# One-hot tiles of eight tokens per VectorE compare in the expert-gate scatter of a PEER block, and the gates as a second pass

## The chip, the cores and the metric

The kernel runs on one core of one Trainium2 chip, in one launch. The metric is the device time of that launch in microseconds (us), the median of repeated runs; lower is better. All data are float32. The engines are TensorE (PE; its weight loads are listed as PEld), VectorE (DVE), ScalarE (ACT), GpSimd (POOL) and SyncE (SP), which issues most DMAs.

## The reference, cut to what matters

The whole model is one block of gated linear attention with a PEER layer and two blocks of attention with a convolutional feed-forward, over 512 tokens of width 1024. The change lies in the PEER layer. For each of 512 tokens, 8 retrieval heads pick 16 experts each out of 128 x 128 = 16,384 by product keys, so that a token has 128 selected experts with a softmax gate each:

```python
expert = (jnp.take_along_axis(i1, top_c // PEER_TOPK, axis=-1) * PEER_N_KEYS
          + jnp.take_along_axis(i2, top_c % PEER_TOPK, axis=-1))
gate = jax.nn.softmax(top_s, axis=-1)
...
act = jax.nn.gelu(jnp.einsum("pd,ped->pe", xb, jnp.take(u, eb, axis=0)), approximate=False)
return jnp.einsum("pe,ped->pd", (gb * act).astype(v.dtype), jnp.take(v, eb, axis=0))
```

An expert's number is e1 * 128 + e2. The kernel treats 384 of the tokens (TD) densely: it computes the activations of all 16,384 experts and multiplies them by a dense matrix of gates, zero for experts not selected. The other 128 tokens are gathered row by row.

## The kernel before, in words

Each engine's program is written out by hand, stage after stage; the engines meet at semaphores (`wait_ge(name, key)`, `inc(name, key)`), and each engine executes its instructions in the written order. `after(stage, ...)` makes an engine wait for the end of a stage on the others. The stages around the change are *retrieve* (queries, key scores, the top-16 searches, expert numbers), *spread* (the stage that is changed) and *experts* (the dense products over 64 blocks of 256 experts).

**The work of the spread stage.** It makes, for each dense token t, the 128 x 128 matrix of its gates. `e1T`, `e2T` and `gT` are 128 x 384 tiles: partition s holds, in column t, the two halves of the number and the gate of the token's s-th selected expert. `iota` holds 0 to 127 along each partition's row. Two one-hot tiles of 128 x 128 are made: `oa` is 1 where iota equals e1T's column t, multiplied by the gate gT; `ob` is 1 where iota equals e2T's column. One float32 matmul of the two, over the 128 selections, gives the token's gates; four tokens share a PSUM bank `B[q % 8]` (q counts groups of four, 96 in all). ScalarE copies each bank into `stage` (written token-last), and SyncE stores a full stage of 32 tokens (BT) to DRAM (`gd`), whence the experts stage loads it (`gt`).

**Who makes what, before.** There are 24 buffers of 128 x 128 for `oa` and 24 for `ob` (NOH). VectorE makes every `oa` in one instruction (compare, then multiply by the gate; two scalar columns). The `ob` of a token goes by `t % 16`: 5 of 16 to ScalarE (two instructions, |iota - e2| and relu(1 - that)), 3 of 16 to VectorE, 8 of 16 to GpSimd. Each instruction signals, TensorE waits for both tiles of a token, and a buffer is free again when the matmul of 24 tokens before is done. ScalarE's order is that of `spread_order()`: the `ob` tiles of four tokens, two groups of four ahead, then the copy of one bank. GpSimd first issues four indirect DMAs (`own_row_pool`, L2185), which wait for the expert numbers of the other 128 tokens.

The neighbouring lines which the text uses: L1908, L1929, L1944 and L1948 are the retrieve stage's broadcast operations of 128 x 1024 elements (`ge`, `eq`), of which VectorE and GpSimd each take some; L196 splits weights; L499 is a VectorE multiply with accumulation, and L2329 is GpSimd's multiply of activations by gates, both in the experts stage. L234 is the common matmul line.

Of the kernel before, what the change touches and what calls it, by code (L numbers as in the profile page):

```python
# [7 lines left out]
ALU = mybir.AluOpType  # L8
ACT = mybir.ActivationFunctionType
# [11 lines left out]
T = TX + TC  # L21
# [8 lines left out]
BT = 32  # L30
# [107 lines left out]
def spread(ap, n):  # L138
    return ap.unsqueeze(2).to_broadcast([ap.shape[0], ap.shape[1], n])
# [1510 lines left out]
TD = 384  # L1650
# [28 lines left out]
def peer_plan(k):  # L1679
    m = k.m  # L1680
    k.U2 = m.pair("Up", [128, KC, TX])
    k.own = Net()
    k.own.x = m.sb("ownx", [128, D])
    k.own.at, k.own.atf = m.sb("ownat", [128, NSLOT], U32), m.sb("ownatf", [128, NSLOT])
    k.own.gate, k.own.dot, k.own.w = (m.sb("own", [128, NSLOT]) for _ in range(3))
    own_u = m.top
    k.own.u = [m.sb("ownu", [128, D]) for _ in range(NUB)]
    top = m.top
    k.n2 = NormMod(k, "n2", k.X, k.sc2, k.MOD[0][:, 24:32, :], k.U2, (XR,), sums_at=own_u, sums=4, rows=3)
    m.top = top  # L1690
    k.peer_top = m.top
    k.iota, k.marks = m.sb("iota", [128, 128]), m.sb("marks", [128, 32])
    k.e1T, k.e2T, k.gT = (m.sb("eT", [128, TD]) for _ in range(3))
    top2 = m.top
    k.R = Retrieval(k)
    m.top = top2
    k.oa = [m.sb("oa", [128, 128]) for _ in range(24)]
    k.ob = [m.sb("ob", [128, 128]) for _ in range(24)]
    k.stage = [m.sb("stage", [128, 128, BT]) for _ in range(2)]
    m.top = top  # L1700
    k.gt = [m.sb("gt", [128, TD // BT, 4, BT]) for _ in range(2)]
    k.acts = [m.pair("act", [128, 2, TD]) for _ in range(2)]
    k.ge = [m.sb("ge", [128, TD]) for _ in range(2)]
    k.own.acc = k.X[:, 0:4, TX:T]
    side = m.top
    k.side = [m.sb("side", [128, TW]) for _ in range(2)]
    k.cb2 = m.sb("cb", [128, 2 * D])
    k.dots3 = Dots(k, "experts", k.cb2, k.X[:, 4:8, TX:T])
    k.own.v = [m.sb("ownv", [128, D]) for _ in range(NVB)]
    end, m.top = m.top, side  # L1710
    k.ot = [m.sb("ot", [128, D]) for _ in range(3)]
    m.top = end
# [341 lines left out]

def expert_engine(t):

    if t % 16 in (1, 5, 7, 11, 13):
        return "act"  # L2060
    return "dve" if t % 16 in (3, 8, 14) else "pool"


NOH = 24


def spread_order():

    out = [("hot", t) for t in range(8)]
    for q in range(TD // 4):  # L2070
        if q + 2 < TD // 4:
            out += [("hot", t) for t in range(4 * q + 8, 4 * q + 12)]
        out.append(("group", q))
    return out


def spread_pe(k):
    pe = k.pe
    for q in range(TD // 4):
        b = k.B[q % 8]  # L2080
        if q >= 8:
            pe.wait_ge("staged", q - 8)
        for i in range(4):
            t = 4 * q + i
            pe.wait_ge("hot_a", t)
            if expert_engine(t) == "act":
                pe.wait_ge("hot_act", t)
            elif expert_engine(t) == "dve":
                pe.wait_ge("hot_dve", t)
            else:  # L2090
                pe.wait_ge("hot_pool", t)
            ins = pe.e.matmul(b[:, i * 128:(i + 1) * 128], k.ob[t % NOH][:], k.oa[t % NOH][:], start=True, stop=True)  # L2092
            ins.then_inc(*pe.inc("mm", ("hot", t)))
    pe.mark("spread")


def spread_act(k):
    a = k.act
    a.after("retrieve", "pe", "dve", "pool")
    for what, t in spread_order():  # L2100
        if what == "hot":
            if expert_engine(t) == "act":
                ob = k.ob[t % NOH]
                if t >= NOH:
                    a.wait_ge("mm", ("hot", t - NOH))
                a.e.activation(ob[:], k.iota[:], ACT.Abs, bias=k.e2T[:, t:t + 1], scale=-1.0).then_inc(*a.inc("hot_act", (t, 0)))
                a.wait_ge("hot_act", (t, 0))
                a.e.activation(ob[:], ob[:], ACT.Relu, bias=k.one[:, 0:1], scale=-1.0).then_inc(*a.inc("hot_act", t))
        else:
            n, i0 = 4 * t // BT, 4 * t % BT  # L2110
            a.wait_ge("mm", ("hot", 4 * t + 3))
            if n >= 2:
                a.wait_ge(f"stored{n % 2}", n - 2)
            a.e.activation(k.stage[n % 2][:, :, i0:i0 + 4], k.B[t % 8].rearrange("p (t i) -> p i t", t=4), ACT.Copy).then_inc(
                *a.inc("staged", t))
    a.mark("spread")


def spread_dve(k):
    v = k.dve  # L2120
    v.after("retrieve", "pe", "act", "pool")
    v.wait_ge("chosen", ("T", 2))
    for t in range(TD):
        if t >= NOH:
            v.wait_ge("mm", ("hot", t - NOH))
        v.e.tensor_scalar(k.oa[t % NOH][:], k.iota[:], k.e1T[:, t:t + 1], k.gT[:, t:t + 1], ALU.is_equal, ALU.mult).then_inc(
            *v.inc("hot_a", t))
        if expert_engine(t) == "dve":
            v.e.tensor_scalar(k.ob[t % NOH][:], k.iota[:], k.e2T[:, t:t + 1], None, ALU.is_equal).then_inc(*v.inc("hot_dve", t))
    v.mark("spread")  # L2130


def spread_pool(k):
    g = k.pool
    g.after("retrieve", "pe", "act", "dve")
    for s in range(NUB):
        own_row_pool(k, "u", s)
    for t in range(TD):
        if expert_engine(t) == "pool":
            if t >= NOH:  # L2140
                g.wait_ge("mm", ("hot", t - NOH))
            g.e.tensor_scalar(k.ob[t % NOH][:], k.iota[:], k.e2T[:, t:t + 1], None, ALU.is_equal).then_inc(*g.inc("hot_pool", t))
    g.mark("spread")


def spread_sp(k):
# [31 lines left out]
def own_row_pool(k, which, s):  # L2178

    g, S = k.pool, k.own  # L2180
    g.wait_ge("own", "at")
    if which == "u":
        if s >= NUB:
            g.wait_ge("own_dot", s - NUB)
        g.e.indirect_dma_start(S.u[s % NUB][:], None, k.dram["un"], bass.IndirectOffsetOnAxis(S.at[:, s:s + 1], 0)).then_inc(  # L2185
            *g.inc(f"own_u{s % NUB}", s, by=16))
    else:
        if s >= NVB:
            g.wait_ge("own_sum", s - NVB)
        g.e.indirect_dma_start(S.v[s % NVB][:], None, k.dram["vn"], bass.IndirectOffsetOnAxis(S.at[:, s:s + 1], 0)).then_inc(  # L2190
            *g.inc(f"own_v{s % NVB}", s, by=16))
# [1813 lines left out]
def tensor_program(k):  # L4005
# [9 lines left out]
    n2_pe(k)  # L4015
    retrieve_pe(k)
    spread_pe(k)
    experts_pe(k)
    join_pe(k)
# [18 lines left out]
def scalar_program(k):  # L4038
# [8 lines left out]
    n2_act(k)  # L4047
    retrieve_act(k)
    spread_act(k)
    experts_act(k)  # L4050
    join_act(k)
# [19 lines left out]
def vector_program(k):  # L4071
# [8 lines left out]
    n2_dve(k)  # L4080
    retrieve_dve(k)
    spread_dve(k)
    experts_dve(k)
    join_dve(k)
# [19 lines left out]
def gpsimd_program(k):  # L4104
# [9 lines left out]
    n2_pool(k)  # L4114
    retrieve_pool(k)
    spread_pool(k)
    experts_pool(k)
    join_pool(k)
# [34 lines left out]
def make_plan(k):  # L4153
# [32 lines left out]
    assert m.top <= heads  # L4186
    m.top = base
    peer_plan(k)
    m.top = base
    k.r64, k.r96 = m.sb("r64", [128, 128]), m.sb("r96", [128, 128])  # L4190
# [247 lines left out]
```

## Time and profile before

| | |
|---|---|
| median of 3 runs | 5478.99 us (5473.9 to 5482.6) |
| the profiled execution | 5479.94 us |
| its span | 5478.6 us |
| granted TensorE clock over the span | 0.951 |
| spread stage: first one-hot to the next stage's first matmul | 1324.43 to 1465.00 us |

Times in the trace count from the span's start. Busy time of an engine is the sum over its instructions. PEclk, the granted clock, is a share of TensorE's full speed of 2.4 GHz; it has two levels, 0.5 and 1.0, and a value between them is a mixture over the stretch. Some instructions of an engine overlap by a fraction of a microsecond, so that the distance from start to start is shorter than the duration.

### The profile page before, as it was taken

The numbers are of one execution on the slowest core, as the hardware profiler recorded it, in microseconds if no ns is written. First come the engines' busy times: TensorE is split into PE (matmuls) and PEld (weight loads), VectorE is DVE, ScalarE is ACT, GpSimd is POOL, SyncE is SP. The second block draws the span as 40 slices with busy tenths as digits, with TensorE's granted clock in tenths as the row PEclk, the third lists the DMA queues.
The fourth block names the chain that finished last, engine by engine and source line by source line (L and its number), as shares of the span: only waits on it lengthen the run. The fifth ranks groups of instructions, "written<-read, shape, count | busy, mean of one in ns | idle before, by whom it ended". The sixth has DMA issues, their size and how long they took to land.

```text
span 5478.6 us, 67230 instructions
## 1 busy us (share of the span) xinstructions
PE 4942.2 (90%) x27217; PEld 4153.0 (76%) x27217; DVE 3122.6 (57%) x5388; ACT 1909.0 (35%) x2822; POOL 1176.5 (21%) x1003
## 2 busy tenths in 40 slices
PE   7998899965899999999789988979999799899999
PEld 7887777754788888888667776768888667777787
DVE  5444455579767777775444555555444544444545
ACT  3445522223733333333341423313222343333333
POOL 1111100025644545442120002200000120021000
PEclk8999999987999999999899999999999899999999
DMA  3111023412588888884103012121111101112221
GB/s 151 52 53 63 24 100 125 152 40 76 228 276 303 305 301 301 303 284 167 55 24 124 28 70 75 61 113 62 58 63 62 44 24 67 39 48 93 78 98 71
DMA packets 157444, 638.39 MB, mean 117 GB/s; under 512 B 12384, under 2 KB 62577, under 8 KB 106321
## 3 DMA queue, kind: packets, MB, share of 16 engines
q1 hardware_dynamic: 112528, 467.97, 24.1%
q0 software_dynamic: 42528, 162.98, 8.5%
q8 instruction: 217, 3.56, 0.3%
q10 hardware_dynamic: 2080, 3.15, 0.2%
q14 instruction: 91, 0.74, 0.0%
HBM read 597.35 MB, written 36.70 MB: 116 GB/s over the span
## 4 chain that ended last, share of the span: by engine, by line
PE 75%; DVE 10%; ACT 7%; issue 3%; DMA 3%; POOL 2%; DVEq 0%; SPq 0%; ACTq 0%; POOLq 0%
PE banks L234 63%; PE banks L2793 2%; PE banks L2892 1%; PE banks L2798 1%; DVE cols L2824 1%; ACT P L2842 1%; PE banks L2919 1%; PE banks L962 1%; DVE raw L499 1%; DVE prod L499 1%; PE banks L355 1%; PE banks L2092 1%; PE banks L308 1%; DMA X<-ctxT_in 1%; PE banks L894 1%
## 5 line engine op out<-in xcount | busy, mean ns | idle before, releaser
L234 PE MATMUL banks<-UH,spl1H 128*128 128x512 f32 (+1 forms) x1600 | 591.6, 370 | 46.6 <-issue 16.7
L196 DVE TENSOR_TENSOR spl0L<-raw,spl0H 128x2048 fp32r<-128x2048 f32 (+3 forms) x171 | 370.9, 2169 | 424.2 <-ACT spl0H L181 377.9
L234 PE MATMUL banks<-UL,spl1H 128*128 128x512 f32 (+1 forms) x1600 | 583.3, 365 | 0.0
L234 PE MATMUL banks<-UH,spl1L 128*128 128x512 f32 (+1 forms) x1600 | 582.4, 364 | 0.0
L196 DVE TENSOR_TENSOR spl1L<-raw,spl1H 128x2048 fp32r<-128x2048 f32 (+1 forms) x170 | 379.2, 2231 | 344.4 <-ACT spl1H L181 341.4
L234 PE MATMUL banks<-UH,spl0H 128*128 128x512 f32 (+2 forms) x1184 | 434.0, 367 | 41.1 <-issue 12.7
L181 ACT ACTIVATE spl1H<-raw 128x2048 fp32r<-128x2048 f32 (+1 forms) x170 | 313.5, 1844 | 440.5 <-PE banks L234 280.8
L181 ACT ACTIVATE spl0H<-raw 128x2048 fp32r<-128x2048 f32 (+3 forms) x171 | 306.2, 1790 | 422.7 <-PE banks L234 202.0
L234 PE MATMUL banks<-UL,spl0H 128*128 128x512 f32 (+2 forms) x1184 | 427.9, 361 | 0.0
L234 PE MATMUL banks<-UH,spl0L 128*128 128x512 f32 (+2 forms) x1184 | 427.2, 361 | 0.0
L234 PE MATMUL banks<-UpH,spl0H 128*128 128x384 f32 (+1 forms) x1072 | 370.7, 346 | 44.2 <-issue 23.0
L234 PEld LDWEIGHTS banks<-UH,spl1H 128*128 128x128 f32 x1600 | 306.0, 191 | 107.1 <-issue 47.3
L234 PE MATMUL banks<-UpL,spl0H 128*128 128x384 f32 (+1 forms) x1072 | 367.8, 343 | 0.0
L234 PE MATMUL banks<-UpH,spl0L 128*128 128x384 f32 (+1 forms) x1072 | 367.6, 343 | 0.0
L234 PEld LDWEIGHTS banks<-UH,spl1L 128*128 128x128 f32 x1600 | 305.9, 191 | 51.7
L234 PEld LDWEIGHTS banks<-UL,spl1H 128*128 128x128 f32 x1600 | 306.4, 191 | 50.4 <-issue 0.8
L234 PE MATMUL banks<-spl1H,actH 128*128 128x512 f32 x756 | 299.4, 396 | 15.5 <-issue 15.5
L2824 DVE TENSOR_REDUCE cols<-banks 128x1 f32<-128x768 f32 (+3 forms) x240 | 190.7, 795 | 189.5 <-PE banks L2798 106.0
L234 PE MATMUL banks<-spl1L,actH 128*128 128x512 f32 x756 | 298.3, 395 | 0.0
L234 PE MATMUL banks<-spl1H,actL 128*128 128x512 f32 x756 | 298.2, 394 | 0.0
L234 PEld LDWEIGHTS banks<-UH,spl0H 128*128 128x128 f32 (+1 forms) x1184 | 225.7, 191 | 87.0 <-issue 38.9
L3962 POOL TENSOR_TENSOR cv<-cv 128x768 f32<-128x768 f32 (+1 forms) x44 | 69.0, 1569 | 922.5 <-DVE cv L3933 922.5
(477 smaller groups left out, 11560.9 us busy)
## 6 DMA issues: line engine op xcount, KB each, us to landing
raw<-uT_in SPq DMA_DIRECT2D x64, 1024.0 KB
raw<-ev_in SPq DMA_DIRECT2D x64, 1024.0 KB
raw<-up_in SPq DMA_DIRECT2D x44, 1024.0 KB
raw<-ada_in SPq DMA_DIRECT2D x40, 1024.0 KB
gd<-stage SPq DMA_DIRECT2D x12, 2048.0 KB, 6.6
gt<-gd SPq DMA_DIRECT2D x32, 768.0 KB, 7.3
side<-ada_in SPq DMA_DIRECT2D x24, 1024.0 KB, 6.6
raw<-gate_in SPq DMA_DIRECT2D x24, 1024.0 KB
```

The costliest lines, as they stand in the source:

```text
L181: a.e.activation(k.spl[i % SPL].h[:, 0:w], k.raw[j % RAW][:, 0:w], ACT.Copy).then_inc(*a.inc("w_hi", j))
L196: v.e.tensor_tensor(s.l[:, 0:w], k.raw[j % RAW][:, 0:w], s.h[:, 0:w].bitcast(F32), ALU.subtract).then_inc(*v.inc("w_lo", j))
L234: ins = pe.e.matmul(out, x, y, start=start and i == 0 and j == 0, stop=stop and i == n - 1 and j == 2)
L308: ins = pe.e.matmul(s.sums[:, o:o + 1], s.sq[i % len(s.sq)][:, c * 128:(c + 1) * 128], k.ones[:, 0:1], start=(i == 0 and c == 0), stop=(j ...
L355: ins = pe.e.matmul(b[:, c * 128:(c + 1) * 128], k.ones[:], d[:, c, :], start=True, stop=True)
L499: v.e.scalar_tensor_tensor(x if r else S.out, x, 1.0, w, ALU.mult, ALU.mult, accum_out=MOD[:, 2 * t + c, r:r + 1]).then_inc(*v.inc("dot", ...
L894: ins = pe.e.matmul(state_at(H, d, gi, c), w.kdT[r:r + 64, c // 2, :], v[r:r + 64, c // 2, :], start=True, stop=True)
L962: ins = pe.e.matmul(o[:, c * 64:(c + 1) * 64], w.S[:, c, x * 128:(x + 1) * 128], w.qd[:, c * 64:(c + 1) * 64], start=False, stop=(c == ord ...
L2092: ins = pe.e.matmul(b[:, i * 128:(i + 1) * 128], k.ob[t % NOH][:], k.oa[t % NOH][:], start=True, stop=True)
L2793: ins = pe.e.matmul(k.W[1 + j][:, at:at + n], Q[lo:hi, q * 128:(q + 1) * 128], K[lo:hi, k0:k0 + n], start=True, stop=True)
L2824: v.e.reduce_max(mx, src, AX_X).then_inc(*v.inc("largest", (tag, i, j)))
L3962: g.e.tensor_tensor(va[:, 0:w], va[:, 0:w], ga[:, 0:w], ALU.mult).then_inc(*g.inc("ffn_prod", (l, j)))
```

## The change

The 24 + 24 small buffers become 3 + 3 buffers of eight tokens each (NHOT, HOT; the same memory). VectorE makes `oa` of eight tokens in one `tensor_tensor` compare of 128 x 1024 elements, both inputs read from SBUF with broadcasts: iota repeated over the eight tokens, e1T's column repeated over 128 elements. The gate is no longer part of it: for 29 of the 48 groups VectorE multiplies `oa` by gT in a second `tensor_tensor`, for the other 19 ScalarE scales the eight pieces in place, one instruction each. `ob` comes from GpSimd for 22 groups (eight `tensor_scalar` instructions as before, one signal behind the eighth) and from VectorE for 26 (one compare of 128 x 1024). ScalarE makes no one-hots any more. TensorE has the same 384 matmuls, waits once for a group of eight, and signals once in four.

```diff
-    k.oa = [m.sb("oa", [128, 128]) for _ in range(24)]
-    k.ob = [m.sb("ob", [128, 128]) for _ in range(24)]
+    k.oa, k.ob = ([m.sb(n, [128, HOT, 128]) for _ in range(NHOT)] for n in ("oa", "ob"))
...
+HOT, NHOT = 8, 3
...
+def second_on_pool(g):
+
+    return g % 2 == 0 and g % 24 != 22
...
+def gates_on_act(g):
+
+    return g % 5 in (1, 3)
...
+def tokens_of(x, g):
+
+    return spread(x[:, g * HOT:(g + 1) * HOT], 128)
...
 def spread_pe(k):
...
+        if gates_on_act(g):
+            pe.wait_ge("hot_act", g)
+        else:
+            pe.wait_ge("hot_gate", g)
+        if second_on_pool(g):
+            pe.wait_ge("hot_pool", g)
+        else:
+            pe.wait_ge("hot_dve", g)
         for i in range(4):
...
+            t = 4 * (q % 2) + i
+            ins = pe.e.matmul(b[:, i * 128:(i + 1) * 128], k.ob[g % NHOT][:, t, :], k.oa[g % NHOT][:, t, :], start=True, stop=True)
+        ins.then_inc(*pe.inc("mm", ("hot", q)))
...
+def gates_act(k, g):
+
+    a = k.act
+    if g < TD // HOT and gates_on_act(g):
+        a.wait_ge("hot_a", g)
+        for t in range(HOT):
+            o = k.oa[g % NHOT][:, t, :]
+            ins = a.e.activation(o, o, ACT.Copy, scale=k.gT[:, g * HOT + t:g * HOT + t + 1])
+        ins.then_inc(*a.inc("hot_act", g))
...
+    for q in range(TD // 4):
+        if q % 2 == 0:
+            gates_act(k, q // 2 + 2)
...
-    for t in range(TD):
-        if t >= NOH:
-            v.wait_ge("mm", ("hot", t - NOH))
-        v.e.tensor_scalar(k.oa[t % NOH][:], k.iota[:], k.e1T[:, t:t + 1], k.gT[:, t:t + 1], ALU.is_equal, ALU.mult).then_inc(
-            *v.inc("hot_a", t))
-        if expert_engine(t) == "dve":
-            v.e.tensor_scalar(k.ob[t % NOH][:], k.iota[:], k.e2T[:, t:t + 1], None, ALU.is_equal).then_inc(*v.inc("hot_dve", t))
+    io = k.iota[:].unsqueeze(1).to_broadcast([128, HOT, 128])
+    for g in range(TD // HOT):
+        oa, ob = k.oa[g % NHOT], k.ob[g % NHOT]
+        if g >= NHOT:
+            v.wait_ge("mm", ("hot", 2 * (g - NHOT) + 1))
+        v.e.tensor_tensor(oa[:], io, tokens_of(k.e1T, g), ALU.is_equal).then_inc(*v.inc("hot_a", g))
+        if not second_on_pool(g):
+            v.e.tensor_tensor(ob[:], io, tokens_of(k.e2T, g), ALU.is_equal).then_inc(*v.inc("hot_dve", g))
+        if not gates_on_act(g):
+            v.wait_ge("hot_a", g)
+            v.e.tensor_tensor(oa[:], oa[:], tokens_of(k.gT, g), ALU.mult).then_inc(*v.inc("hot_gate", g))
...
+    for g in range(TD // HOT):
+        if second_on_pool(g):
+            if g >= NHOT:
+                p.wait_ge("mm", ("hot", 2 * (g - NHOT) + 1))
+            for t in range(HOT):
+                ins = p.e.tensor_scalar(k.ob[g % NHOT][:, t, :], k.iota[:], k.e2T[:, g * HOT + t:g * HOT + t + 1], None, ALU.is_equal)
+            ins.then_inc(*p.inc("hot_pool", g))
```

VectorE's instructions from the start of the spread stage on, before (line, operation, output and inputs, elements, count in a row; `eT` is any of e1T, e2T and gT):

```order
L2126 TENSOR_SCALAR oa<-iota,eT 128x128 x4
L2129 TENSOR_SCALAR ob<-iota,eT 128x128
L2126 TENSOR_SCALAR oa<-iota,eT 128x128 x5
L2129 TENSOR_SCALAR ob<-iota,eT 128x128
L2126 TENSOR_SCALAR oa<-iota,eT 128x128 x6
L2129 TENSOR_SCALAR ob<-iota,eT 128x128
```

VectorE's instructions at the same place in the changed kernel:

```order
L2133 TENSOR_TENSOR oa<-iota,eT 128x1024
L2138 TENSOR_TENSOR oa<-oa,eT 128x1024
L2133 TENSOR_TENSOR oa<-iota,eT 128x1024
L2135 TENSOR_TENSOR ob<-iota,eT 128x1024
L2133 TENSOR_TENSOR oa<-iota,eT 128x1024
L2138 TENSOR_TENSOR oa<-oa,eT 128x1024
```

The first six rows held 15 + 3 instructions on 128 x 128 elements, one tensor input each; now six instructions with two tensor inputs each cover the groups 0 to 2, which are 24 tokens. The group 1 has its gates from ScalarE, the groups 0 and 2 their `ob` from GpSimd.

ScalarE's instructions from the start of the stage on, before:

```order
L2106 ACTIVATE ob<-iota,eT 128x128
L2108 ACTIVATE ob<-ob,one 128x128
L2106 ACTIVATE ob<-iota,eT 128x128
L2108 ACTIVATE ob<-ob,one 128x128
L2106 ACTIVATE ob<-iota,eT 128x128
L2108 ACTIVATE ob<-ob,one 128x128
L2106 ACTIVATE ob<-iota,eT 128x128
L2108 ACTIVATE ob<-ob,one 128x128
L2114 ACTIVATE stage<-banks 128x128x4
```

And in the changed kernel:

```order
L2102 ACTIVATE oa<-oa,eT 128x128 x8
L2119 ACTIVATE stage<-banks 128x128x4 x2
L2102 ACTIVATE oa<-oa,eT 128x128 x8
L2119 ACTIVATE stage<-banks 128x128x4 x6
L2102 ACTIVATE oa<-oa,eT 128x128 x8
```

The pairs that made `ob` are gone; eight scalings in a row stand ahead of every fourth or sixth copy of a bank.

## Rows read from the trace of the kernel before

**Rows 1.** Windows: busy us and count by engine, then granted clock, DMA share.

```profile
core 0: us, PE busy (x) PEld busy (x) DVE busy (x) ACT busy (x) POOL busy (x), PEclk, DMA share, GB/s
1340.00:1360.00 20.00, 16.99 (x116) 14.24 (x116) 19.46 (x74) 19.41 (x51) 20.00 (x33) 1.00 0.44 182
```

**Rows 2.** Groups of instructions, 1324 to 1466 us: busy us, mean ns, idle before.

```profile
L2142 POOL TENSOR_SCALAR ob<-iota,eT 128x128 f32<-128x128 f32 x192 | 121.5, 646 | 4.9 <-PE banks L2092 4.6
L2126 DVE TENSOR_SCALAR oa<-iota,eT 128x128 f32<-128x128 f32 x384 | 115.9, 358 | 7.3 <-PE banks L2092 6.2
L2114 ACT ACTIVATE stage<-banks 128x512 f32<-128x512 f32 x96 | 55.4, 579 | 6.6 <-PE banks L2092 6.5
L2129 DVE TENSOR_SCALAR ob<-iota,eT 128x128 f32<-128x128 f32 x72 | 21.5, 299 | 0.0
```

**Rows 3.** Timeline, one period of 16 tokens on TensorE: start, length, count.

```profile
1374.53 5.03 PE L2092 MATMUL banks<-oa,ob 128*128 128x128 f32 x32 [0.52 <-ACT ob L2108]
1380.09 5.03 PE L2092 MATMUL banks<-oa,ob 128*128 128x128 f32 x32 [0.53 <-ACT ob L2108]
1457.83 0.97 PEld L2092 LDWEIGHTS banks<-oa,ob 128*128 128x128 f32 x8 [0.69 <-issue]
```

**Rows 4.** Timeline at the start and the end of the spread stage.

```profile
1324.43 1.11 DVE L2126 TENSOR_SCALAR oa<-iota,eT 128x128 f32<-128x128 f32 x4
1324.91 0.40 ACT L2108 ACTIVATE ob<-ob,one 128x128 f32<-128x128 f32 x1
1325.21 0.39 ACT L2106 ACTIVATE ob<-iota,eT 128x128 f32<-128x128 f32 x1
1330.27 20.14 POOL L2142 TENSOR_SCALAR ob<-iota,eT 128x128 f32<-128x128 f32 x32
1463.17 1.78 ACT L2114 ACTIVATE stage<-banks 128x512 f32<-128x512 f32 x3
1465.00 0.44 PE L234 MATMUL banks<-UpH,spl1H 128*128 128x384 f32 x1 [0.69 <-ACT stage L2114]
```

**Rows 5.** Timeline, VectorE and GpSimd operations of 128 x 1024 in retrieve.

```profile
1307.10 1.21 DVE L1929 TENSOR_TENSOR eq<-small,iota 128x1024 f32<-128x1024 f32 x1
1308.22 1.21 DVE L1935 TENSOR_REDUCE ex<-eq 128x64 f32<-128x1024 f32 x1
1308.39 2.34 POOL L1948 TENSOR_TENSOR eq<-eq,small 128x1024 f32<-128x1024 f32 x1 [6.19 <-DVE eq L1929]
1309.35 2.46 DVE L1908 TENSOR_TENSOR ge<-small,marks 128x1024 f32<-128x1024 f32 x1
1317.28 1.16 DVE L1929 TENSOR_TENSOR eq<-small,iota 128x1024 f32<-128x1024 f32 x1
1318.48 1.23 DVE L1948 TENSOR_TENSOR eq<-eq,small 128x1024 f32<-128x1024 f32 x1
```

**Rows 6.** Timeline, GpSimd behind a VectorE operation; then both in the experts stage.

```profile
1277.49 2.28 DVE L196 TENSOR_TENSOR spl1L<-raw,spl1H 128x2048 fp32r<-128x2048 f32 x1
1277.64 4.33 POOL L1944 TENSOR_TENSOR ge<-ge,small 128x1024 f32<-128x1024 f32 x1 [1.16 <-DVE ge L1908]
...
2452.87 1.22 DVE L499 SCALAR_TENSOR_TENSOR X<-side,cb 128x1024 f32<-128x1024 f32 x1
2452.87 2.09 POOL L2329 TENSOR_TENSOR ge<-ge,gt 128x384 f32<-128x384 f32 x1 [1.02 <-ACT ge L2294]
2454.12 1.91 DVE L499 SCALAR_TENSOR_TENSOR side<-side,cb 128x1024 f32<-128x1024 f32 x1
```

**Rows 7.** Instructions by line: durations ns min/median/max, first and last start.

```profile
L2142 POOL TENSOR_SCALAR ob<-iota,eT x192: 592/636/827, 1330.3 to 1456.0; 128x128 f32<-128x128 f32 x192
L2129 DVE TENSOR_SCALAR ob<-iota,eT x72: 273/301/395, 1325.5 to 1455.8; 128x128 f32<-128x128 f32 x72
L1944 POOL TENSOR_TENSOR ge<-ge,small x7: 2337/4357/4422, 1158.3 to 1299.9; 128x1024 f32<-128x1024 f32 x7
```

**Rows 8.** Windows of the retrieve stage: busy us by engine, granted clock.

```profile
1150.00:1200.00 50.00, 37.18 (x162) 30.37 (x160) 43.86 (x250) 10.58 (x20) 18.53 (x22) 0.83 0.12 43
```

## What the change does to the time, forecast from the trace

> **What bounds the kernel now.** I looked first at the stage that is touched. It runs from VectorE's first one-hot at 1324.43 to the next stage's first matmul at 1465.00 [rows 4]: 140.6 us, 2.6% of the span. Outside it the change alters nothing but line numbers, so the whole effect lies in when that last matmul starts. Then the windows: in 20 us of steady state ScalarE is busy 19.41, VectorE 19.46, GpSimd 20.00 and TensorE 16.99 [rows 1]. Three engines are full at once, and that is the first thing to see: no engine can be relieved alone. The timeline shows who ends the waits: the 16-token pattern repeats after 1380.09 - 1374.53 = 5.56 us, and each new period on TensorE begins at an `ob` of ScalarE [rows 3]; 24 periods are 133.4 us. The rest is the start, where GpSimd compares only from 1330.27 on, behind its four indirect DMAs [rows 4]. TensorE itself could be quicker: the eight weight loads of four tokens take 0.97 us when nothing holds them up [rows 3], so 384 tokens need some 93 us.
>
> **ScalarE.** Its 240 one-hot instructions go. It gets 19 x 8 = 152 scalings; like instructions follow each other after 1325.21 - 1324.91 = 0.30 us [rows 4], which is 46 us, and the bank copies stay at 55.4 us [rows 2]. Together 101 us in a stage of 140: it stops being the bound. The work goes to VectorE.
>
> **VectorE by itself.** Its 384 + 72 instructions, 137.4 us of overlapping durations [rows 2], become 48 + 26 compares and 29 multiplies of 128 x 1024, 103 in all. The price is shown by the same shapes with the same broadcasts: from a compare to an independent instruction 1308.22 - 1307.10 = 1.12 us, and 1318.48 - 1317.28 = 1.20 us to a multiply that waits for that compare [rows 5]. So 74 x 1.12 + 29 x 1.20 = 117.7 us if nothing disturbs it. That is nearly what its part of the stage is now; the eightfold instruction saves little, since the gate becomes a second pass.
>
> **VectorE against GpSimd: the term that decides.** The old VectorE instructions read one tensor, the new ones two. Wherever a VectorE instruction with two inputs in SBUF meets a GpSimd `tensor_tensor`, the trace shows one of them standing still. The `ge` compare began at 1309.35 under a GpSimd multiply that ended at 1308.39 + 2.34 = 1310.73, and took 2.46 us, ending 1.08 after it; the reduction under the same multiply took its plain 1.21 [rows 5]. The other way round, GpSimd's multiply began at 1277.64 under a VectorE subtraction that ended at 1279.77, and ended 2.20 us later, where the fastest of its kind takes 2.337 in all [rows 6, 7]: only 0.14 us was hidden. In the experts stage they alternate: GpSimd ends 0.87 after VectorE, and VectorE's next 1.07 after GpSimd [rows 6]. Such pairs add up instead of overlapping.
>
> That is what the Trainium skill says in "SBUF — State Buffer", under "Who interferes with whom": a VectorE instruction with two SBUF inputs contends with a GpSimd instruction that reads SBUF, and the pair of ports is held for the whole instruction. The rows just read agree, for `tensor_tensor` on GpSimd. By the rule the sum would be the upper of the two below.
>
> No row shows a GpSimd `tensor_scalar`, of which 22 x 8 = 176 remain, against two inputs on VectorE. Its cost is bounded from both sides. Upper: it shuts VectorE out as its `tensor_tensor` does, for 0.592 [rows 7] less the hidden 0.14, 0.45 us. Lower: the one-input compares of VectorE that share the stage with exactly these GpSimd instructions, which fill all of the stretch [rows 1], range from 273 to 395 ns [rows 7], so they never waited more than 0.12 us. Nothing at all is a rival of its own (below).
>
> Now the sum. Up to 1330.3 GpSimd issues DMAs and VectorE gets 5 instructions done (5.9 us at 1.12 to 1.20); 98 remain. As long as both have work they take turns, since each waiting one is served when the other ends: one GpSimd instruction per VectorE instruction, 1.08 + h us. That handles 98 of GpSimd's 176; the other 78 run while VectorE waits for a buffer, at 0.60 us each (between the least, 0.592, and the median, 0.636 [rows 7]), 46.8 us. VectorE does have to wait: the ring has three groups, group g + 3 needs the matmuls of g, and those need GpSimd's eight pieces. GpSimd seldom waits, since its next group is g + 2, in the buffer of g - 1.
>
> - h = 0.45: 98 x 1.53 + 46.8 = 196.7, the last one-hot at 1527.0.
> - h = 0.12: 98 x 1.20 + 46.8 = 164.4, at 1494.7.
>
> Behind it come eight matmuls, 2 x 0.97 = 1.9 us, and the last copy of a bank, 1.78 / 3 = 0.6 us [rows 3, 4], with signals 3 us, against 1465.00 now: +65 and +33 us. The row on the very instruction speaks for short, those on two inputs for long; with nothing nearer I take the middle, h = 0.29: 98 x 1.37 + 46.8 = 181.1, next stage at 1514.4, +49 us. Startup costs nothing beyond this: group 0 is complete when GpSimd has made eight pieces, and TensorE has slack. Fewer signals and waits on TensorE are costed at nothing, being covered by the same wait for one-hots; if the cover were gone, the floor of 93 us is still far below.
>
> The profiled execution is 5479.94, 1 us above the median of the runs. 5479.9 + 49 = 5529 against that execution, and 5528 against the median of 5478.99.
>
> **The rivals.**
>
> 1. *No contention with `tensor_scalar`* (ends on the other side). For it: GpSimd's 192 compares now run with a median of 636 against a least of 592 ns beside a full VectorE [rows 7], although some of VectorE's are slowed. Against it: GpSimd's operand comes through the same memory as its `tensor_tensor`'s. VectorE's 117.7 us then are the bound. At the start it is ahead by three groups at about 1331.3 and waits for group 0: 1330.3 + 8 x 0.60 + 1.9 = 1337.0, 6 us idle. The next stage starts at 1324.4 + 117.7 + 6 + 3 = 1451, 14 us earlier; GpSimd needs 4.8 of each 4.9 us for 16 tokens, so part of it may go in ring waits. 5466 to 5480. It decides if GpSimd shuts VectorE out for less than some 0.02 us per instruction. Chance 0.14: faster 0.08, same 0.06.
> 2. *GpSimd is stopped twice in an instruction*, once for the scalar column and once for the row, and gets through one in two VectorE instructions. Then 49 are done beside the 98, and 127 alone: 98 x 1.20 + 127 x 0.60 = 193.8 (+62 us) to 98 x 1.53 + 76.2 = 226.1 (+95 us). All that speaks for it is the long duration of each (0.592 us for 128 elements); no row shows two stops. 5541 to 5574. Chance 0.12.
> 3. *TensorE becomes the bound at the lower clock level.* Its bursts of 1.9 us would fill 3.9 of 7.5 us per 16 tokens, half; in retrieve, at 37.18 us busy of 50, the granted clock was 0.83, a mixture of both levels [rows 8]. At 1.2 GHz throughout, 16 tokens take 4 x 2 x 0.97 = 7.8 us, 24 times 186 us: about +55 us. It hides under the main forecast and adds some 5 us. Chance 0.06.
> 4. *Little changes*: VectorE's turns cost about h = 0.12, and two GpSimd instructions fit between two of VectorE's, so that the 78 alone shrink to few: 98 x 1.2 + 10 = 128 to 140, -2 to +12 us. 5478 to 5491. Chance 0.06: same 0.04, slower 0.02.
>
> **How the numbers follow.** The main case, one GpSimd instruction per VectorE instruction and an added wait between the bounds, has 0.62: 5512 to 5545. It and rivals 2 and 3 are slower throughout, as is a third of rival 4. Two kernels of this length can be told apart from about 0.2%, 11 us. That gives faster 0.08, same 0.10, slower 0.82. The range goes from 5475, which takes in rival 4 and the upper half of rival 1, to 5565, two thirds of rival 2: about 0.1 is left out below and 0.05 above.
>
> **What the profile would show.** Right: VectorE's 128 x 1024 compares in the stage with a median well above 1.22 us (1.3 to 1.7), and GpSimd's compares above 0.64, up to 1.5 us; the sum of VectorE's and GpSimd's busy time inflated by waits; TensorE busy at about half in the stage, its waits ended by GpSimd's `ob`; ScalarE idle a third of it. The stage 174 to 206 us long, all other stages as they were. Wrong: VectorE's compares at 1.2 and GpSimd's at 0.6 side by side, which is rival 1; GpSimd's at over 1.7 us, rival 2. The forecast also fails if the two do not take turns, one of them holding the other off for long runs; then the sum stays but the split between the two kinds of wait changes.

## The result, and the profile after

The changed kernel takes 5552.23 us (median of 4 runs, 5546.34 to 5552.93) against 5479.42 us: a ratio of 1.0136, 95% interval 1.0120 to 1.0152. The forecast was 5528 with a range to 5565: right in direction, and 24 us short in size. 5552 lies outside the 5512 to 5545 of the main case and inside the 5541 to 5574 of rival 2.

The stage, from the windows of the profile after (columns as in [rows 1]), and the waits of the stage (who waited for whom: us in total, times, longest us):

```profile
core 0: us, PE busy (x) PEld busy (x) DVE busy (x) ACT busy (x) POOL busy (x), PEclk, DMA share, GB/s
1361.00:1381.00 20.00, 12.78 (x91) 12.62 (x90) 12.99 (x12) 10.36 (x27) 18.88 (x18) 0.74 0.25 106
```

```profile
PE banks L2090 <- POOL ob L2152: 92.2, 13, 13.5
DVE oa L2133 <- PE banks L2090: 84.6, 15, 9.5
ACT oa L2102 <- DVE oa L2133: 36.4, 19, 12.4
POOL ob L2152 <- PE banks L2090: 17.0, 10, 6.5
```

Where three engines were full [rows 1], GpSimd alone is nearly so now (18.88 of 20 us). TensorE waits 92.2 us for its one-hots, VectorE 84.6 us for TensorE to free a buffer; VectorE and ScalarE are idle a third and a half of the time. The stage ran from 1324.51 to 1536.47 us, 211.96 in place of 140.57 [rows 4]: 71.4 of the 72.8 us by which the span grew. The rest of the kernel took 0.1 us more ahead of the stage and 1.3 us more behind it.

The groups of the stage after, against [rows 2]:

```profile
L2152 POOL TENSOR_SCALAR ob<-iota,eT 128x128 f32<-128x128 f32 x176 | 176.5, 1024 | 17.0 <-PE banks L2090 17.0
L2133 DVE TENSOR_TENSOR oa<-iota,eT 128x1024 f32<-128x1024 f32 x48 | 59.0, 1235 | 84.8 <-PE banks L2090 84.6
L2138 DVE TENSOR_TENSOR oa<-oa,eT 128x1024 f32<-128x1024 f32 x29 | 36.0, 1243 | 0.5
L2135 DVE TENSOR_TENSOR ob<-iota,eT 128x1024 f32<-128x1024 f32 x26 | 33.8, 1300 | 0.0
```

Fewer GpSimd compares than before (176 for 192) are busy for longer (176.5 for 121.5 us), while VectorE's are hardly above their 1.21 us. Read one by one, VectorE and GpSimd in the same 5 us:

```profile
1346.45 1.21 DVE L2133 TENSOR_TENSOR oa<-iota,eT 128x1024 f32<-128x1024 f32 x1
1347.58 1.30 DVE L2135 TENSOR_TENSOR ob<-iota,eT 128x1024 f32<-128x1024 f32 x1
1348.81 1.21 DVE L2138 TENSOR_TENSOR oa<-oa,eT 128x1024 f32<-128x1024 f32 x1
1349.95 1.30 DVE L2133 TENSOR_TENSOR oa<-iota,eT 128x1024 f32<-128x1024 f32 x1
```

```profile
1345.67 2.38 POOL L2152 TENSOR_SCALAR ob<-iota,eT 128x128 f32<-128x128 f32 x1
1348.03 2.38 POOL L2152 TENSOR_SCALAR ob<-iota,eT 128x128 f32<-128x128 f32 x1
```

A GpSimd compare ends every 2.36 us, one for two VectorE instructions, and every second VectorE instruction is 0.09 us longer. The compare that began at 1345.67 outlasted the instruction that VectorE was in (to 1346.52) and the whole next one (to 1347.66), and ended 0.39 us after that. Over the 176 records: 52 lasted over 1.3 us, together 105.4 us; the other 124 took 0.60 each, 74.7 us. With 17.0 us of waits, less 3.7 us by which neighbours overlap, that is the 193.4 us from the first to the last (1332.5 to 1525.9). It is rival 2, counted beforehand as 49 beside VectorE and 127 alone.

### The profile page after: what moved, and what is told of

It is laid out like the page before. It is cut to its first block, busy times and chain, and to the rows that moved or that the text cites. A ratio compares the mean times of both kernels' runs of the same rounds, so it can differ in the third digit from the quotient of the medians.

```text
span 5551.4 us, 66438 instructions
## 1 busy us (share of the span) xinstructions
PE 4947.1 (89%) x27217; PEld 4173.1 (75%) x27217; DVE 3121.5 (56%) x5035; ACT 1877.3 (34%) x2734; POOL 1233.0 (22%) x987
## 4 chain that ended last, share of the span: by engine, by line
PE 78%; DVE 8%; ACT 6%; POOL 4%; issue 3%; DMA 2%; DVEq 0%; ACTq 0%; POOLq 0%; SPq 0%
PE banks L234 64%; POOL ob L2152 2%; PE banks L2804 2%; PE banks L2903 1%; PE banks L2809 1%; PE banks L2090 1%; ACT P L2853 1%; DVE cols L2835 1%; PE banks L2930 1%; PE banks L962 1%; PE banks L308 1%; PE banks L355 1%; DMA X<-ctxT_in 1%; PE banks L894 1%; PE banks L953 1%
```

## The experiments

Theory A: a VectorE instruction with two inputs in SBUF keeps GpSimd out while it runs. Theory B: the hand-over of eight tokens in a ring of three groups costs the time. The stage's length below goes from VectorE's first one-hot to the next stage's first matmul, as in [rows 4]. The kernel before was run again beside the experiments: medians of 5473.84, 5473.88 and 5473.88 us, and 5474.09 in the single run that belongs to the constant for the scalar column. That is 5 to 6 us below the 5479.42 beside the changed kernel, so differences in total between experiments are taken from each one's own kernel before (the changed kernel: 72.8 us above). Where no ratio is given, the experiment is a single run and is judged by its stage.

**One input, by scalar columns.**

```diff
-        v.e.tensor_tensor(oa[:], io, tokens_of(k.e1T, g), ALU.is_equal).then_inc(*v.inc("hot_a", g))
+        v.e.tensor_scalar(oa[:], io, k.e1T[:, g * HOT:g * HOT + 1], k.one[:, 0:1], ALU.is_equal, ALU.mult).then_inc(*v.inc("hot_a", g))
...
```

> The changed kernel, but VectorE's instructions of the stage read one tensor in place of two: compares and gate multiplies of 128 x 1024 take scalar columns (one of the group's first token, one of ones). Left out: all eight tokens of a group get the first one's column. Theory A (a second SBUF input on VectorE keeps GpSimd out of its reads): GpSimd's compares at 0.60 us with none over 0.8, its indirect DMA issues back at 0.95 us, VectorE's instructions about 1.2 us, the stage 126 to 132 us in place of 211, total 5465 to 5475. Theory B (the coarse hand-over of eight tokens in a ring of three groups costs the time, whoever reads what): the stage stays above 190 us, total above 5530.

5503.75 us, the stage 164.9 us: neither. The edit changed more than it was meant to:

```profile
L2133 DVE TENSOR_SCALAR oa<-iota,eT,one x48: 799/816/1222, 1327.1 to 1485.9; 128x1024 f32<-128x1024 f32 x48
L2152 POOL TENSOR_SCALAR ob<-iota,eT x176: 590/597/1717, 1333.2 to 1483.1; 128x128 f32<-128x128 f32 x176
```

VectorE read 1024 elements in 0.80 us instead of 1.21, and 63 GpSimd compares lasted over 0.7 and up to 1.72 us. So one input is not enough to leave GpSimd alone. The Trainium skill, "VectorE: DVE Perf Modes", section "Mode 2×_2P — use both read ports for one tensor", says that an instruction with one tensor input can read the two halves of that tensor through both read ports at once, on float32 too; the 0.80 us agree. As a test of the second input the run decides nothing.

**One input, at the same 1.21 us.**

```diff
-        v.e.tensor_tensor(oa[:], io, tokens_of(k.e1T, g), ALU.is_equal).then_inc(*v.inc("hot_a", g))
+        if g < NHOT:
+            v.e.tensor_tensor(oa[:], io, tokens_of(k.e1T, g), ALU.is_equal).then_inc(*v.inc("hot_a", g))
+        else:
+            v.e.tensor_reduce(oa[:, :, 0], io, AX_X, ALU.add).then_inc(*v.inc("hot_a", g))
...
```

> The changed kernel, but from group 3 on each VectorE instruction of the stage is a reduction over the same 128 x 1024 elements of iota, which reads one tensor, one element per cycle, and writes eight elements per partition. Left out: the compares and multiplies of these groups. Theory A: with the same 1.2 us instructions but one input, GpSimd's compares stay at 0.60 us, none above 0.8 after group 2; stage 120 to 131 us, some 10 us below the kernel before. In the run with one input and scalar columns VectorE's instructions fell to 0.81 us, two elements per cycle, and GpSimd was still held up; if it is VectorE's being busy with long instructions as such that holds GpSimd up, here too a third of its compares last over 1.3 us and the stage stays above 165 us.

5467.72 us, the stage 131.8 us, 1 us beyond the forecast's end:

```profile
L2136 DVE TENSOR_REDUCE oa<-iota x45: 1209/1210/1222, 1342.0 to 1450.9; 128x8 f32<-128x1024 f32 x45
L2163 POOL TENSOR_SCALAR ob<-iota,eT x176: 590/607/652, 1333.4 to 1446.0; 128x128 f32<-128x128 f32 x176
```

The same 1.21 us on VectorE, the same ring and groups of eight, and no GpSimd compare above 0.652. So VectorE's being busy does not hold GpSimd up, and theory B falls. The reduction differs in what it writes, too, so by itself this does not yet name the second input.

**The second input from PSUM.** The whole computation is kept.

```diff
+RING = (0, 1, 3, 4, 5, 6, 7)
...
-        b, g = k.B[q % 8], q // 2
-        if q >= 8:
-            pe.wait_ge("staged", q - 8)
+        b, g = k.B[RING[q % 7]], q // 2
+        if q >= 7:
+            pe.wait_ge("staged", q - 7)
...
-    io = k.iota[:].unsqueeze(1).to_broadcast([128, HOT, 128])
+    v.e.tensor_copy(k.B[2][:, TD:TX], k.iota[:]).then_inc(*v.inc("iota_bank", 0))
+    v.wait_ge("iota_bank", 0)
+    io = k.B[2][:, TD:TX].unsqueeze(1).to_broadcast([128, HOT, 128])
...
-            v.e.tensor_tensor(oa[:], oa[:], tokens_of(k.gT, g), ALU.mult).then_inc(*v.inc("hot_gate", g))
+            v.e.tensor_tensor(oa[:], oa[:], tokens_of(k.B[2], g), ALU.mult).then_inc(*v.inc("hot_gate", g))
```

> The changed kernel, computing all of it, but VectorE's second input comes from PSUM: iota is copied to the last quarter of bank 2 and the gates are read where the transposes left them in the same bank; the four-token results go round the other seven banks. Theory A (only a second input from SBUF keeps GpSimd out): GpSimd's compares at 0.60 us beside 1.2 us instructions of VectorE, the stage 124 to 132 us, total 8 to 16 us below the kernel before. If GpSimd is still held up, the stage stays near 200 us.

5468.55 us, ratio to the kernel before 0.9986 (0.9976 to 0.9996); the stage 129.1 us.

```profile
L2136 DVE TENSOR_TENSOR oa<-banks,eT x48: 1210/1216/1225, 1326.3 to 1449.1; 128x1024 f32<-128x1024 f32 x48
L2141 DVE TENSOR_TENSOR oa<-oa,banks x29: 1206/1212/1222, 1327.6 to 1451.4; 128x1024 f32<-128x1024 f32 x29
L2155 POOL TENSOR_SCALAR ob<-iota,eT x176: 590/607/642, 1331.8 to 1444.1; 128x128 f32<-128x128 f32 x176
```

The same instructions of the same length with the same writes; what differs is where one input lies (and that the results go round seven banks, which cannot shorten the stage by itself), and 83 us of stage are gone. This shows the cause: the second input from SBUF. The total misses its forecast of 8 to 16 us below the kernel before by little: 5 us by the medians, 8 by the ratio.

**GpSimd writes only.**

```diff
-                ins = p.e.tensor_scalar(k.ob[g % NHOT][:, t, :], k.iota[:], k.e2T[:, g * HOT + t:g * HOT + t + 1], None, ALU.is_equal)
+                ins = p.e.memset(k.ob[g % NHOT][:, t, :], 1.0)
```

> The changed kernel, with GpSimd's compares replaced by memsets of the same 128 x 128 tiles, which read nothing. Left out: the second one-hots of 22 groups. Theory A with reads as the contended part: no memset is held up, all at one duration below 0.3 us, although VectorE is as busy as before; the stage near 125 us and 5465 to 5475. If writes contend as well, some of them last 1 to 2.4 us, as GpSimd's compares do in the changed kernel (52 of 176 above 1.3 us).

5471.73 us, the stage 129.0 us:

```profile
L2152 POOL MEMSET ob<- x176: 204/207/219, 1334.7 to 1441.4; 128x128 f32 x176
```

All 176 alike beside VectorE's two-input instructions, which filled 19.3 to 19.9 of each 20 us: it is GpSimd's reads that are shut out. The section of the Trainium skill's "SBUF — State Buffer" that the prediction drew on, "Who interferes with whom", says this too, that a GpSimd instruction that only writes does not contend; 0.219 us at most agrees.

**A constant for the scalar column.**

```diff
-                ins = p.e.tensor_scalar(k.ob[g % NHOT][:, t, :], k.iota[:], k.e2T[:, g * HOT + t:g * HOT + t + 1], None, ALU.is_equal)
+                ins = p.e.tensor_scalar(k.ob[g % NHOT][:, t, :], k.iota[:], float(t), None, ALU.is_equal)
```

> The changed kernel, with GpSimd's compares taking a constant of the instruction instead of a scalar column of e2T. Left out: the right second one-hots of 22 groups. It tells why a GpSimd compare loses two VectorE instructions. If it is stopped once for the column and once for the row, it is now stopped once: the longest last about 1.3 us in place of 2.38. If both stops belong to the row (a read and then something else through the same port), the longest stay near 2.3 us. Either way the total falls, since alone such an instruction is shorter (0.84 us for 768 elements with constants).

5530.42 us, the stage 192.7 us. GpSimd at the place where the changed kernel's took 2.38:

```profile
1346.19 1.26 POOL L2152 TENSOR_SCALAR ob<-iota 128x128 f32<-128x128 f32 x1
1347.42 1.26 POOL L2152 TENSOR_SCALAR ob<-iota 128x128 f32<-128x128 f32 x1
```

One VectorE instruction per compare in place of two: 78 of 176 were held up (94.5 us in all). So one of the two stops goes with the scalar column. The other is then most likely the reading of the row: a memset, which reads nothing, is not stopped. No run took the row away alone.

**VectorE's instructions in halves and quarters.**

```diff
+        for hf in range(2):
+            hs = slice(hf * 4, hf * 4 + 4)
+            xs = tokens_of(k.e1T, g)[:, hs, :]
+            ins = v.e.tensor_tensor(oa[:, hs, :], io[:, hs, :], xs, ALU.is_equal)
+        ins.then_inc(*v.inc("hot_a", g))
...
```

> The changed kernel, with each VectorE instruction cut in two of 128 x 512, everything else as it is. Theory A in the form that a GpSimd compare is held up by two VectorE instructions whatever their length: the longest GpSimd compares fall from 2.38 to about 1.3 us, 98 rather than 49 are done beside VectorE, the rest alone: some 15 us less than the changed kernel, 5530 to 5542. If GpSimd is let in only when VectorE's queue pauses, its longest compares grow beyond 2.4 us and the total stays at 5552 or above. Theory B: no change beyond VectorE's added overhead, 5550 to 5560.

5535.40 us, ratio 1.0111 (1.0095 to 1.0128), the stage 198.0 us. In total it is 61.6 us above the kernel before, 11 less than the changed kernel; the forecast was some 15 less. A held-up compare in the steady stretch:

```profile
1348.35 1.31 POOL L2164 TENSOR_SCALAR ob<-iota,eT 128x128 f32<-128x128 f32 x1
```

Two instructions 0.65 us apart, as forecast: 90 were held up in place of 52, each for half as long.

> The changed kernel, with each VectorE instruction cut in four of 128 x 256. Theory A, two VectorE instructions per held-up GpSimd compare: its longest compares fall to 0.8 us or less, nearly all 176 fit beside VectorE, whose own 412 instructions at some 0.34 us take 140 us and now bound the stage, 150 to 165 us; total 8 to 25 us above the kernel before, against 78 for the changed kernel and 62 for halves.

5518.63 us in one run, 45 us above the kernel before, and the stage 179.7 us, 15 us beyond the forecast's end.

```profile
L2136 DVE TENSOR_TENSOR oa<-iota,eT x192: 408/416/700, 1322.2 to 1495.9; 128x256 f32<-128x256 f32 x192
L2164 POOL TENSOR_SCALAR ob<-iota,eT x176: 590/863/1142, 1328.3 to 1490.1; 128x128 f32<-128x128 f32 x176
```

The forecast had 0.8 us at most; of the 147 compares longer than 0.7 us, 95 took some 0.86 us and 47 some 1.12, which is 2.5 to 3.3 VectorE instructions at 0.34 us from start to start. The compare of 1345.88 to 1347.00 outlasted two of them, like the long ones, and ended 0.38 us after the second (1346.62), by when a third was over but for 0.04 us. So the stops are still two, as far as this compare shows; what the forecast left out are these last 0.38 us, which are small beside 1.2 us and more than a whole instruction here. That this part of the compare needs no turn of its own is read from the trace and was not tested.

**One GpSimd instruction per group.** The eight compares of a group are replaced by one `tensor_tensor` of 128 x 1024 on GpSimd, a product; the 22 second one-hots are left out.

```diff
-            for t in range(HOT):
-                ins = p.e.tensor_scalar(k.ob[g % NHOT][:, t, :], k.iota[:], k.e2T[:, g * HOT + t:g * HOT + t + 1], None, ALU.is_equal)
+            ins = p.e.tensor_tensor(k.ob[g % NHOT][:], k.iota[:].unsqueeze(1).to_broadcast([128, HOT, 128]), tokens_of(k.e2T, g), ALU.mult)
```

> [...] Alone such an instruction takes 2.34 us against 8 x 0.60. Theory A with the exclusion seen in retrieve: VectorE waits for all of it, 22 x 2.2 us added to VectorE's 111 us, the stage about 165 us and 25 us above the kernel before. If GpSimd shuts VectorE out for only 0.09 us, as its tensor_scalar does in the changed kernel, the stage is near 130 us and the total below the kernel before.

5500.43 us, 27 us above the kernel before, the stage 162.4 us for a forecast of 165.

```profile
1354.38 2.49 POOL L2151 TENSOR_TENSOR ob<-iota,eT 128x1024 f32<-128x1024 f32 x1 [7.16 <-PE banks L2090]
1355.04 2.91 DVE L2133 TENSOR_TENSOR oa<-iota,eT 128x1024 f32<-128x1024 f32 x1
```

GpSimd ended at 1356.87, VectorE at 1357.95, 1.08 later: here VectorE waits for all of GpSimd's instruction, as in [rows 5]. The stage is 33 us longer than the 129.1 of the second input from PSUM, where the changed kernel's 176 compares cost 83.

**Without GpSimd.**

```diff
 def second_on_pool(g):
-    return g % 2 == 0 and g % 24 != 22
+    return False
```

> The changed kernel, with all second one-hots on VectorE and none on GpSimd: 125 VectorE instructions of 128 x 1024. Theory A: 96 x 1.13 + 29 x 1.20 = 143 us, the stage about 146, total 5479 + 6 = 5485 (5480 to 5492), GpSimd's help having been worth less than nothing. Theory B: the ring still stalls VectorE for tens of us, total above 5500.

5479.21 us, ratio 1.0009 (1.0000 to 1.0019), the stage 144.8 us. With 22 more compares on VectorE the stage is 67 us shorter than the changed kernel's, and so is the total, each against its own kernel before (5 us above it in place of 73): GpSimd's help cost more than it gave. ScalarE was busy 12.71 of 20 us, so gates were moved to it (`return g % 3 != 0` in `gates_on_act`):

> As no_pool, but ScalarE applies the gates of 32 groups in place of 19. VectorE has 96 + 16 = 112 instructions, 96 x 1.13 + 16 x 1.20 = 128 us; ScalarE 32 x 2.4 + 96 x 0.5 = 125 us. Theory A: both nearly full, the stage 130 to 140 us in place of 144.8, total 0 to 10 us below the kernel before. If the hand-over of groups between the engines costs the rest (theory B in a weaker form), no change against no_pool.

5470.36 us, ratio 0.9993 (0.9984 to 1.0002), the stage 132.6 us. The stage shortened as forecast; against the kernel before, the total can't be told from no change.

**Two versions that follow from it.** Both are iota_in_psum with `gates_on_act` returning `g % 2 == 1`; the second has also `return g % 2 == 0 and g > 0` in `second_on_pool`.

> As iota_in_psum, with ScalarE applying the gates of the 24 odd groups in place of 19. VectorE has 98 instructions: 74 x 1.13 + 24 x 1.20 = 112 us, ScalarE 24 x 2.4 + 96 x 0.5 = 106, GpSimd 176 x 0.60 = 106 from 1330 us on. Theory A: nothing adds up any more, the busiest engine sets the end, the stage 120 to 126 us in place of 129, total 14 to 20 us below the kernel before.

5465.27 us, ratio 0.9983 (0.9974 to 0.9992), the stage 125.1 us, in its range; the gain of 9 us is below the 14 to 20 forecast.

> As psum_gates_odd, but group 0 has its second one-hots from VectorE and GpSimd makes those of the 23 other even groups, so that TensorE need not wait for the four indirect DMAs and eight GpSimd compares at the start. VectorE 99 instructions, 113 us with no idle start: the stage 116 to 121 us, total 20 to 26 us (0.4 to 0.5 per cent) below the kernel before. If GpSimd's 184 compares from 1330 us on, 110 us, are what ends last, no gain over psum_gates_odd.

5458.38 us, ratio 0.9971 (0.9960 to 0.9981), 16 us below the kernel before, for 20 to 26 forecast; the stage 117.1 us, as forecast. Its windows:

```profile
1370.00:1390.00 20.00, 16.68 (x143) 16.03 (x142) 19.83 (x18) 18.88 (x53) 20.00 (x36) 1.00 0.57 238
```

VectorE and GpSimd are full side by side, and the granted clock is at its upper level of 2.4 GHz. It is faster than both kernels, by 3 in a thousand against the kernel before. A stage 23.5 us shorter goes with 16 us of total, but the two do not compare the same executions: the traced one of the kernel before took 5479.94 us, 6 us more than that kernel's median here. Between the two traces the spans differ by 23.2 us (5478.6 and 5455.4), as the stages do. Outside the stage the traced executions took between 5333 and 5342 us, whatever the kernel, so that one trace can't settle a few us of total.

## Why the prediction came out as it did

- *The bound before.* ScalarE, VectorE and GpSimd full together: not tested by itself. The relief of ScalarE came as computed (forecast 101 us of work; measured 46.5 + 53.1 = 99.6 us).
- *VectorE by itself,* 117.7 us: right. With the second input in PSUM, where nothing contends, the stage is 129.1 us for the 126.6 of rival 1, and VectorE waited once, 6.9 us, for the 6 of rival 1.
- *The term that decides,* contention with a GpSimd instruction that no row showed: right that it exists, and that it goes with the second input. The sum's form was wrong in one step: "one GpSimd instruction per VectorE instruction, 1.08 + h us". Measured: one per two, and h = 0.09 on every second one. The two errors have opposite signs, fewer GpSimd compares hidden and a smaller added wait, which is why the total came out only 24 us short; that it fell into the range is owed to rival 2, for which the range had been drawn wide, and not to the main case, given 0.62. The middle, h = 0.29, stood on nothing; the row on the very instruction (0.12 at most) was near the truth, the full exclusion by rows of `tensor_tensor` was not. The rule of the Trainium skill's "SBUF — State Buffer", section "Who interferes with whom", an exclusive hold for the whole instruction, holds for VectorE's side and for GpSimd's `tensor_tensor`, but GpSimd's `tensor_scalar` of 0.60 us shut VectorE out for only 0.09.
- *Rival 2,* two stops per GpSimd instruction, given 0.12, is what happened, and the run with a constant showed that one of the stops goes with the column. Its sum with h = 0.12 was 193.8 us from 1330.3 on, +62 us. Measured: 193.4 us, but from 1332.5 on, +71 us. 2.2 of the missing 9 us are the indirect DMAs of the start (below); most of the rest is the tail: from GpSimd's last compare (1525.94) to the next stage's first matmul (1536.47) it took 10.5 us where the sum had 3 for eight matmuls. That compare belongs to group 44, and the 32 tokens of the groups 44 to 47 were still to be multiplied; group 47's one-hots waited for a buffer until 1529.87. Against the +49 us that were forecast, the 22 us that are missing are 12 of taking turns (193.4 for 181.1), 2 of the start and 7.5 of the tail.
- *TensorE at the lower clock level* (rival 3): the granted clock was 0.74 in the steady stretch, between the levels, behind 12.78 of 20 us busy. TensorE waited 92 us for GpSimd, so most of it hid under that, as said. In the tail it did not: the last 64 matmuls took 9.70 us at a granted clock of 0.76, for 8 x 0.97 = 7.8 us by [rows 3], an estimate of 2 us.
- *Startup costs nothing:* wrong by 2.2 us, since GpSimd began its compares at 1332.51 in place of 1330.27.
- *What the profile would show:* GpSimd's compares "above 0.64, up to 1.5 us" and VectorE's at "1.3 to 1.7" named the wrong one of the two as the one that waits. 2.38 us is what the text gave as the sign of rival 2, "over 1.7 us". The stage, 212 us, is beyond the 174 to 206 given, and ScalarE was idle for half of it rather than a third.

## What to carry to other kernels

Before VectorE's instructions are merged into larger ones with a second tensor input, ask what GpSimd does beside them. Here a GpSimd compare with a scalar column that met them was stopped for two VectorE instructions (2.38 us in place of 0.60; 52 of 176 were held up), and many short compares beside long two-input instructions gave the longest stage of all. Halves, quarters and one long GpSimd instruction each took part of that back. What took back all of it was one of VectorE's inputs in PSUM, for one copy of iota (0.29 us) and one of the eight banks in the ring; the gates lay there already. Leaving GpSimd out and giving ScalarE more gates did nearly as well (132.6 us of stage for 129.1). And where a wait has no row for its pair of instructions, ask how often in one instruction it can strike before taking a middle between bounds.

## What was not expected of the hardware

The indirect DMA issues on GpSimd took longer as well: under two-input VectorE instructions of 1.2 us from SBUF two of the four at the start took 1.95 to 1.99 us, for 0.94 to 1.12 in the kernel before and 0.94 to 1.06 with the input in PSUM. That set GpSimd's first compare back from 1330.27 to 1332.5:

```profile
1326.96 1.99 POOL L2196 DMA_INDIRECT ownu<-un_in,ownat  x1 [0.30 <-issue]
1329.26 1.95 POOL L2196 DMA_INDIRECT ownu<-un_in,ownat  x1 [0.30 <-issue]
```

With VectorE's instructions in halves, also with both inputs in SBUF, the four took 1.30, 0.95, 0.94 and 0.93 us. So the second input alone does not hold them up, and what in them waits stays open.

A VectorE `tensor_tensor` of 128 x 1024 took the same 1.21 us with an input in PSUM as with both in SBUF. And a one-input `tensor_scalar` with two scalar columns ran 1024 elements in 0.80 us, though on 128 elements it is 0.06 us slower than the form with one column.
